# A two-block model on one core: the convolved stage with features on the partitions, norm factors spread along tokens, new forget gates, shared weight units, parameters behind the first chunk

## The chip, the cores and the metric

The kernel is one program on 1 core of one Trainium2 chip. TensorE (PE) multiplies, VectorE (DVE) and ScalarE (ACT) work on its results and prepare the weights, GpSimd (POOL) and SyncE (SP) issue most of the DMAs. The metric is device microseconds from start to end of an execution. Before the change the median of 3 runs is 1928.38 us (1926.94 to 1928.7).

## The reference, cut to what matters

A sequence of 256 tokens with 1024 features passes through two layers of a first block and two layers of a second. All data is float32.

- A layer of the first block: RMS norm, a projection to 3072 columns, attention in two kinds (4 differential heads, 8 plain heads), a projection back, and then the **convolved stage**: `u = causal_dwconv(rms_norm(x) @ w_up)`, with three taps along the tokens for each of 2 x 2816 features, split into gate and up, and `x + (silu(g) * up) @ w_down`.
- A layer of the second block: a plain gated stage (`x + 0.5 * (silu(h @ w_gate) * (h @ w_up)) @ w_down`, 2816 wide), a mixer (queries, keys, values, a recurrent unit, gates) and a second plain gated stage. In the mixer eight columns of the projection are the **forget gates**: `log_f = log_sigmoid(h @ w_f + b_f)`, one number for each token and head.

The RMS norm is `x * rsqrt(mean(x*x) + eps) * g`. The kernel multiplies `x` by `g` ahead of the product and by the token's factor (`rstd`) behind it.

## The kernel before, in words

**Products.** Every large product is done in three passes of a rounded format: an operand is split into a rounded part (`_hi`) and what is left (`_lo`), and `three` (L449 to L452) issues hi x hi, hi x lo and lo x hi into one PSUM region. 304 weight units of 1 MB stream in by DMA through three slots of `raw` (`slot` and its callers, L306 to L330); ACT rounds each half unit to `w_hi` (`hi`, L1240 to L1250) and DVE subtracts to `w_lo` (`lo`). There are six half slots; `part_done` of the half unit six back frees one. PE waits for `lo_ready`.

**Orientation.** `quarter` holds 128 tokens x 128 features of the normed input as the stationary operand and streams 512 weight columns; tokens are on the partitions of the result, and a chunk of 512 features takes two banks, one for each half of the tokens. A chunk's product is 16 tiles x 3 matmuls, in four parts. `narrow` does the last chunk of a stage (256 features, 48 matmuls of 256 columns) from a unit of its own, one for gate and one for up.

**The convolved stage** (`ffn_conv` on each engine). Six steps `j`: gate chunk, up chunk, down product of the step before. The gate chunk leaves PSUM on ACT times `rstd` (`copy_gate`, L1395), the up chunk on DVE (`copy_up`, L2176). PE transposes both so that features lie on the partitions (`turn_conv`, L557: 88 transposes in a layer). ACT takes bias and last tap from the transposed bank (`main`, L1405), DVE adds the two others (`taps`, L2188), then ACT's silu, DVE's product, and a hi and a lo for the down product.

**The plain stage** (`ffn_plain`) has silu on ACT and the product on DVE with tokens on the partitions, and transposes the product alone (`turn_prod`, L546).

**The forget gates** (`forget_logits`): for each half of the tokens and each of 8 feature tiles three matmuls with the input as the stationary operand and 8 weight columns streaming, 48 in a layer, between two parts of the mixer's first chunk.

**Stage borders.** `turn_x` (L511) transposes `x` into banks, ACT's `norm_hi` (L1265) and DVE's `norm_lo` (L2035) scale and split it. The first four tiles are turned at the end of a stage, four more at the start of the next. ACT also squares `x` (`squares_x`, L1274).

**The start.** Parameters lie in rows, are loaded by 15 small DMAs and turned on PE (`turn_params`, L918).

**Order.** Nothing is scheduled at run time. The order of every engine's queue is written out by hand, call by call; an engine works through its queue in order, so a call that waits holds back all behind it.

Of the kernel before, what the change touches and what calls it, by code (L numbers as in the profile page):

```python
# [6 lines left out]
F32 = mybir.dt.float32  # L7
# [6 lines left out]
P = 128  # L14
# [30 lines left out]

C1_ATTN, C1_FFN, C1_SUB, C1_QK, C1_CONV, C1 = 0, 8, 16, 17, 21, 197
C2_FFN1, C2_MIX, C2_FFN2, C2_BREST, C2_QN, C2_KN = 0, 8, 16, 40, 72, 73
C2_CB, C2_BA, C2_BX, C2_LAM, C2_CONV, C2_POS, C2 = 74, 82, 90, 98, 106, 138, 146

K_ID, K_TRI, K_ONEU, K_MASK, K_N = 0, 128, 256, 512, 768  # L50
# [36 lines left out]
def build_program(nc, a, out):  # L87
    with ExitStack() as ctx:
# [23 lines left out]
        wf_hi = sb("wf_hi", [P, LAYERS, KT, H2], F32R)  # L112
        wf_lo = sb("wf_lo", [P, LAYERS, KT, H2], F32R)
# [28 lines left out]
        us = stage[:, 1024:2048].rearrange("p (t c) -> p t c", t=TB)  # L142
# [6 lines left out]
        def staged(n):  # L149
# [43 lines left out]
        gs_ready, us_ready, turned_c = sem("gs_ready"), sem("us_ready"), sem("turned_c")  # L193
# [17 lines left out]
        f_done, f_abs, f_exp, f_ready, f_summed, f_copied, decay_ready = (  # L211
            sem("f_done"), sem("f_abs"), sem("f_exp"), sem("f_ready"), sem("f_summed"), sem("f_copied"),
# [14 lines left out]
        rel_done, rel_ready, wf_rounded, lam_sum, lam_exp, lam_in, lam_log = (  # L227
            sem("rel_done"), sem("rel_ready"), sem("wf_rounded"), sem("lam_sum"), sem("lam_exp"), sem("lam_in"),
# [8 lines left out]
        def half0(where):  # L237


            block, layer = where  # L240
            return 23 * layer if block == 1 else 23 * LAYERS + 50 * layer
# [48 lines left out]
        def conv_banks(j):  # L290

            return (C, E) if j == 0 else (A, B)

# [3 lines left out]
        def _(sp):  # L297
# [23 lines left out]
            def narrow(u, w, col):  # L321

                slot(u, w.rearrange("(k p) m -> p k m", p=P)[:, :, col:col + 256], KT)
# [4 lines left out]
            def ffn(u0, gate, up, up_col, down):  # L328
                for j in range(STEPS):
# [4 lines left out]
                    else:  # L334
                        narrow(u0 + ug, gate, CW * j)
                        narrow(u0 + uu, up, up_col + CW * j)
# [40 lines left out]
        def _(pool):  # L377
            nc.gpsimd.memset(eps[:, :], EPS).then_inc(eps_set, 1)
            pool.dma_start(onehot, a["const_onehot"]).then_inc(ld_rel, 16)
# [68 lines left out]
        def _(pe):  # L448
# [39 lines left out]
            def narrow(u, banks, t):  # L488

                pe.wait_ge(lo_ready, 2 * u + 2)  # L490
                for k in range(KT):
                    s, c = (2 * u + k // 4) % NH, 256 * (k % 4)
                    mm = three(bank[banks + t][:, 0:256], r_hi[:, k, t * P:(t + 1) * P], r_lo[:, k, t * P:(t + 1) * P],
                               w_hi[:, s, c:c + 256], w_lo[:, s, c:c + 256], k == 0, k == KT - 1)
                    if t and k % 4 == 3:
                        mm.then_inc(part_done, 1)
                if t == 0:
                    mm.then_inc(half_done, 1)

# [50 lines left out]
            def turn_conv(f, j, up, b):  # L550

                src, ready = (us, us_ready) if up else (gs, gs_ready)
                pe.wait_ge(ready, 12 * f + 2 * j + 2)
                for i in range(2):
                    for t in range(TB):
                        c = (2 * b + i) * P
                        mm = pe.transpose(bank[conv_banks(j)[up] + b][:, i * SEQ + t * P:i * SEQ + (t + 1) * P],  # L557
                                          src[:, t, c:c + P], ident)
                mm.then_inc(turned_c, 1)
# [7 lines left out]
            def ffn_plain(where, n, f, u0):  # L567
                def gate_part(j, i):
# [3 lines left out]
                    if j == STEPS - 1:  # L572
                        free(i)
# [88 lines left out]
            def ffn_conv(where, n, f, u0):  # L662
                def chunk_part(j, up, i):
                    def free(t):
# [3 lines left out]
                        elif j > 1:  # L668
                            pe.wait_ge(conv_done, 22 * f + 4 * (j - 1) + 2 * up + t + 1)
# [2333 lines left out]
```

## Time and profile before

| | |
|---|---|
| runs, median (range) | 1928.38 us (1926.94 to 1928.7) |
| profiled execution | 1928.72 us, span 1926.9 us, mean granted clock 0.993 |
| PE busy | 1892.6 us, 98% |
| DVE busy | 1200.8 us, 62% |
| ACT busy | 1094.6 us, 57% |
| POOL busy | 39.7 us, 2% |
| DMA | 340.86 MB, mean 177 GB/s |

The span is what the trace covers; 1.8 us of the execution lie outside it. A matmul's duration in the trace runs on beyond the start of the next, since they are pipelined: what one costs is the time from its start to the next one's start.

### The profile page before, as it was taken

How to read it: one execution, taken by the hardware profiler on the slowest of the kernel's cores; microseconds unless marked ns; L12 is line 12 of the kernel's file. 1: busy time of each engine (PE TensorE's matmuls, PEld its weight loads, DVE VectorE, ACT ScalarE, POOL GpSimd, SP SyncE). 2: the span in 40 equal slices, each digit the busy share in tenths (PEclk: the TensorE clock that was granted, in tenths of full speed). 3: DMA queues.
4: the chain of work that ended last, by engine and by line, in shares of the span. 5: the costliest groups of instructions: out<-in, count | busy, mean ns of one | idle time of the engine just before them, and what ended most of it. 6: DMA issues, size and time to landing. Idle time of an engine off the chain costs nothing.

```text
span 1926.9 us, 23554 instructions
## 1 busy us (share of the span) xinstructions
PE 1892.6 (98%) x9148; PEld 1575.3 (82%) x9148; DVE 1200.8 (62%) x1767; ACT 1094.6 (57%) x1590; POOL 39.7 (2%) x61
## 2 busy tenths in 40 slices
PE   7999999989999999999999999999999999999999
PEld 6878888878888888888878788888888887888888
DVE  6767768576777655457865554454454686664544
ACT  6766555775646534459864544454444796545442
POOL 2000000000000000000000100000000001000000
PEclk9999999999999999999999999999999999999999
DMA  6535445445554555544555555455553445544553
GB/s 220 186 131 197 154 174 197 153 150 167 186 208 156 183 197 192 175 144 167 179 204 175 175 198 195 168 188 207 178 185 122 174 163 198 187 166 172 204 191 108
DMA packets 157578, 340.86 MB, mean 177 GB/s; under 512 B 5990, under 2 KB 18891, under 8 KB 156955
## 3 DMA queue, kind: packets, MB, share of 16 engines
q1 hardware_dynamic: 154208, 327.24, 49.0%
q0 software_dynamic: 2800, 11.91, 2.0%
q8 instruction: 73, 1.20, 0.3%
q14 instruction: 38, 0.31, 0.0%
q10 hardware_dynamic: 459, 0.20, 0.0%
HBM read 338.24 MB, written 1.09 MB: 176 GB/s over the span
## 4 chain that ended last, share of the span: by engine, by line
PE 89%; DVE 5%; ACT 2%; DMA 2%; issue 1%; POOL 1%; DVEq 0%; ACTq 0%; POOLq 0%
PE bank L450 28%; PE bank L452 27%; PE bank L451 27%; DVE w_lo L2011 2%; PE bank L557 1%; PE bank L546 1%; PE bank L772 1%; DMA t<-by_key 1%; PE bank L1027 1%; ACT w_hi L1250 1%; DMA raw<-in_ffn_w_gate 1%; ACT tmp L1530 1%; PE bank L511 1%; DVE tmp L2347 0%; PE bank L816 0%
## 5 line engine op out<-in xcount | busy, mean ns | idle before, releaser
L2011 DVE TENSOR_TENSOR w_lo<-raw,w_hi 128x1024 fp32r<-128x1024 f32 x620 | 730.2, 1220 | 216.6 <-ACT w_hi L1250 210.3
L1250 ACT ACTIVATE w_hi<-raw 128x1024 fp32r<-128x1024 f32 x620 | 631.3, 1055 | 303.1 <-PE bank L452 172.7
L450 PE MATMUL bank<-w_hi,r_hi 128*128 128x512 f32 (+1 forms) x1792 | 691.2, 386 | 1.5 <-DVE r_lo L2035 1.4
L452 PE MATMUL bank<-w_hi,r_lo 128*128 128x512 f32 (+1 forms) x1792 | 680.6, 380 | 0.0
L451 PE MATMUL bank<-w_lo,r_hi 128*128 128x512 f32 (+1 forms) x1792 | 679.9, 379 | 0.0
L450 PEld LDWEIGHTS bank<-w_hi,r_hi 128*128 128x128 f32 x1792 | 339.1, 189 | 67.0 <-issue 2.5
L452 PEld LDWEIGHTS bank<-w_hi,r_lo 128*128 128x128 f32 x1792 | 338.7, 189 | 64.3
L451 PEld LDWEIGHTS bank<-w_lo,r_hi 128*128 128x128 f32 x1792 | 339.2, 189 | 60.1
L450 PE MATMUL bank<-w_hi,z_hi 128*128 128x512 f32 x656 | 259.0, 395 | 1.7 <-DVE w_lo L2011 1.7
L452 PE MATMUL bank<-w_hi,z_lo 128*128 128x512 f32 x656 | 256.0, 390 | 0.0
L451 PE MATMUL bank<-w_lo,z_hi 128*128 128x512 f32 x656 | 255.4, 389 | 0.0
L450 PEld LDWEIGHTS bank<-w_hi,z_hi 128*128 128x128 f32 x656 | 123.2, 188 | 27.1 <-DVE w_lo L2011 2.1
L452 PEld LDWEIGHTS bank<-w_hi,z_lo 128*128 128x128 f32 x656 | 123.1, 188 | 26.1
L451 PEld LDWEIGHTS bank<-w_lo,z_hi 128*128 128x128 f32 x656 | 123.3, 188 | 24.4
L2073 DVE SCALAR_TENSOR_TENSOR qk<-bank,rstd,stage 128x512 f32<-128x512 f32 (+1 forms) x48 | 33.9, 706 | 132.4 <-PE bank L452 131.8
L2188 DVE SCALAR_TENSOR_TENSOR qk<-bank,par,qk 128x254 f32<-128x254 f32 (+1 forms) x176 | 72.6, 475 | 63.3 <-ACT qk L1405 63.0
L1284 ACT ACTIVATE z_hi<-bank 128x512 fp32r<-128x512 f32 x44 | 25.5, 589 | 148.7 <-PE bank L546 148.7
L1296 ACT ACTIVATE stage<-bank,rstd 128x512 f32<-128x512 f32 (+1 forms) x48 | 31.2, 650 | 102.0 <-PE bank L452 101.9
L1405 ACT ACTIVATE qk<-bank,par 128x256 f32<-128x256 f32 x88 | 43.9, 561 | 67.9 <-PE bank L557 67.9
L2011 DVE TENSOR_TENSOR z_lo<-bank,z_hi 128x512 fp32r<-128x512 f32 x52 | 35.2, 687 | 58.1 <-ACT z_hi L1284 53.4
L2035 DVE SCALAR_TENSOR_TENSOR r_lo<-bank,par,r_hi 128x256 fp32r<-128x256 f32 x80 | 34.4, 478 | 43.9 <-ACT r_hi L1265 43.7
L450 PE MATMUL bank<-w_hi,y_hi 128*128 128x512 f32 x128 | 50.9, 398 | 0.4 <-issue 0.4
(208 smaller groups left out, 1399.0 us busy)
## 6 DMA issues: line engine op xcount, KB each, us to landing
raw<-in_w_in SPq DMA_DIRECT2D x79, 1024.0 KB, 5.3
raw<-in_w_up SPq DMA_DIRECT2D x44, 1024.0 KB, 5.3
raw<-in_ffn_w_gate SPq DMA_DIRECT2D x44, 1024.0 KB, 5.2
raw<-in_ffn_w_up SPq DMA_DIRECT2D x44, 1024.0 KB, 5.7
raw<-in_ffn_w_down SPq DMA_DIRECT2D x44, 1024.0 KB, 5.3
raw<-in_w_down SPq DMA_DIRECT2D x22, 1024.0 KB, 5.0
raw<-in_w_out SPq DMA_DIRECT2D x16, 1024.0 KB, 5.0
raw<-in_w_o_rnn SPq DMA_DIRECT2D x8, 1024.0 KB, 5.0
```

The lines of the kernel that those rows point to most:

```text
L450: pe.matmul(out_, lh, rh, start=start, stop=False, skip_group_check=True)
L451: pe.matmul(out_, lh, rl, start=False, stop=False, skip_group_check=True)
L452: return pe.matmul(out_, ll, rh, start=False, stop=stop, skip_group_check=True)
L511: mm = pe.transpose(x_tile(where, n, k)[:, t * P:(t + 1) * P], x[:, t, k * P:(k + 1) * P], ident)
L1250: A_(w_hi[:, n % NH, :], raw[:, u % NS, HALF * h:HALF * (h + 1)], ACT.Copy).then_inc(hi_ready, 1)
L1284: A_(z_hi[:, tiles, :], src, ACT.Copy).then_inc(g_hi_ready, 1)
L1296: A_(gs[:, t, 0:width], bank[pair_of(j) + t][:, 0:width], ACT.Silu, scale=rstd[:, t:t + 1]).then_inc(silu_ready, 1)
L1405: last = A_((cg, cu)[up][:, tile, :], bank[conv_banks(j)[up] + b][:, i * SEQ:(i + 1) * SEQ], ACT.Identity, bias=kinds[:, 0, up, 4 * j + ti ...
L2011: return V.tensor_tensor(dst, src, hi.bitcast(F32), ALU.subtract)
L2035: V.scalar_tensor_tensor(out=r_lo[:, k, :], in0=x_tile(where, n, k), scalar=gain[:, k:k + 1], in1=r_hi[:, k, :].bitcast(F32), op0=ALU.mult ...
L2073: V.scalar_tensor_tensor(out=prod[:, t, 0:width], in0=bank[pair_of(j + 1) + t][:, 0:width], scalar=rstd[:, t:t + 1], in1=gs[:, t, 0:width] ...
L2188: ks.append(own.link(V.scalar_tensor_tensor(out=dst, in0=bank[conv_banks(j)[up] + b][:, i * SEQ:(i + 1) * SEQ - tap], scalar=kinds[:, kind ...
```

## The change

- In the convolved stage `quarter_rows` takes the place of `quarter` and `narrow`: 128 weight columns are the stationary operand and the 256 tokens stream. A bank holds two feature tiles x 256 tokens; a chunk is 32 tiles x 3 matmuls. The result has features on the partitions, so `turn_conv`, `copy_gate` and `copy_up` go.
- `rstd` is one number for each token and lies on partitions; `spread_factors` turns it so that it lies along the tokens on every partition (2 transposes), DVE copies that to SBUF, and DVE's `scale` multiplies each bank by it into the staging tile. ACT's `main` and DVE's `taps` read that tile and not PSUM.
- The last chunk's gate and up columns share two units in all six gated stages (`pairs`: two DMAs for a unit), and are computed as one 512-column chunk. `narrow` goes.
- The forget gates' 8 weight columns are the first of a stationary operand of 128 columns (what follows in memory fills the rest), the 256 tokens stream: 24 matmuls in a layer. ACT copies 8 rows, PE turns them back in two transposes. They stand one part later in the queue.
- At the start `turn_params(0)` stands behind the first four tiles of `x`, the others partly behind the first chunk, and the rounding of the first weights ahead of the norm.
- At the stage borders the order of squares, norm tiles, weight halves and first products is changed, and many calls in the attention, the mixer and the plain stage change places with neighbours.

```diff
+SHARED = {f0 + 28 + half for half in range(2) for f0 in ...}
-    return (6 * j - 2, 6 * j, 6 * j + 2) if j < STEPS - 1 else (28, 29, 30)
+    return (6 * j - 2, 6 * j, 6 * j + 2) if j < STEPS - 1 else (28, 28, 30)
...
+            def quarter_rows(u, half, n, banks, ready=None, free=None):
+                def tile(m, kk):
+                    k = 4 * half + kk
+                    s, c = (2 * u + kk // 2) % NH, CW * (kk % 2) + P * m
+                    return three(bank[banks + m // 2][:, SEQ * (m % 2):SEQ * (m % 2) + SEQ], w_hi[:, s, c:c + P],
+                                 w_lo[:, s, c:c + P], r_hi[:, k, :], r_lo[:, k, :], k == 0 and m % 2 == 0, k == KT - 1)
+                if half == 0:
+                    pe.wait_ge(lo_ready, 2 * u + n + 1)
+                    for kk in (2 * n, 2 * n + 1):
+                        for m in range(4):
+                            mm = tile(m, kk)
+                    mm.then_inc(part_done, 1)
+                else:
...
+                    for kk in range(4):
+                        for m in (2 * n, 2 * n + 1):
+                            mm = tile(m, kk)
+                        if n and kk % 2:
+                            mm.then_inc(part_done, 1)
+                    if n == 0:
+                        mm.then_inc(half_done, 1)
+
+            def spread_factors(where, n, f):
+                pe.wait_ge(rstd_ready, norm_at(where, n) + 1)
+                for t in range(TB):
+                    mm = pe.transpose(bank[C][:, t * P:(t + 1) * P], rstd[:, t:t + 1].broadcast_to([P, P]), ident)
+                mm.then_inc(spread, 1)
...
                 def forget_logits():
+                    for k in range(KT):
+                        c = (l * KT + k) * H2
+                        mm = three(bank[C][:, 0:256], wf_hi[:, c:c + P], wf_lo[:, c:c + P], r_hi[:, k, :], r_lo[:, k, :],
+                                   k == 0, k == KT - 1)
+                    mm.then_inc(f_done, 1)
-                        for k in range(KT):
-                            mm = three(bank[C][:, t * H2:(t + 1) * H2], r_hi[:, k, t * P:(t + 1) * P],
-                                       r_lo[:, k, t * P:(t + 1) * P], wf_hi[:, l, k, :], wf_lo[:, l, k, :],
...
+                def copy_factors():
+                    dve.wait_ge(spread, f + 1)
+                    own.link(V.tensor_copy(factors, bank[C][:, 0:SEQ]))
+                def scale(j, up, b):
...
+                        dve.wait_ge(conv_main, 22 * f + 4 * (j - 1) + 2 * up + b + 1)
+                    V.tensor_tensor((gf, uf)[up][:, b, :, :], src[:, :].rearrange("p (i s) -> p i s", i=2),
+                                    factors.unsqueeze(1).broadcast_to([P, 2, SEQ]), ALU.mult).then_inc(scaled, 1)
...
 # DVE, convolved stage, steps 2 to 4
                 for j in range(2, STEPS - 1):
+                    scale(j, 0, 0)
                     lo(uj, 0)
-                    prod_lo(j - 1, 0)
                     lo(uj, 1)
                     lo(uj + 1, 0)
                     lo(uj + 1, 1)
+                    prod_lo(j - 1, 0)
+                    prod_lo(j - 1, 1)
+                    lo(uj + 2, 0)
+                    scale(j, 0, 1)
+                    lo(uj + 2, 1)
+                    scale(j, 1, 0)
+                    lo(uj + 3, 0)
+                    scale(j, 1, 1)
+                    lo(uj + 3, 1)
                     taps(j, 0, 0)
...
 # PE, end of the convolved stage
                 last_half(u0, f, 1, 1, 0)
+                turn_next(where, n, 0)
                 last_half(u0, f, 1, 1, 1)
-                turn_next(where, n, 0)
...
 # PE, start of a plain and of a convolved stage
+                gate_part(0, 0)
                 turn_x(where, n, 4)
-                gate_part(0, 0)
...
 # ACT, start of a plain stage
-                hi(u0 + 2, 0)
+                squares_x(where, n, 0)
                 norm_hi(where, n, 0)
                 norm_hi(where, n, 1)
                 norm_hi(where, n, 2)
+                hi(u0 + 2, 0)
                 norm_hi(where, n, 3)
...
 # PE, start of the program
                 x_first(0)
-                turn_params(0)
                 x_first(1)
                 x_first(2)
                 x_first(3)
+                turn_params(0)
                 turn_params(1)
```

## Rows read from the trace of the kernel before

**Rows 1.** The page: busy time of each engine, share of the span, instructions
```profile
PE 1892.6 (98%) x9148; PEld 1575.3 (82%) x9148; DVE 1200.8 (62%) x1767; ACT 1094.6 (57%) x1590; POOL 39.7 (2%) x61
PE 89%; DVE 5%; ACT 2%; DMA 2%; issue 1%; POOL 1%; DVEq 0%; ACTq 0%; POOLq 0%
```
**Rows 2.** Timeline, PE: start us, duration us, what; first and 46th 512-column matmul of a run
```profile
199.80 0.39 PE L452 MATMUL bank<-w_hi,r_lo 128*128 128x512 f32 x1
...
210.00 0.39 PE L452 MATMUL bank<-w_hi,r_lo 128*128 128x512 f32 x1
```
**Rows 3.** Timeline, PE: first and 53rd 256-column matmul of a run
```profile
300.31 0.28 PE L450 MATMUL bank<-w_hi,r_hi 128*128 128x256 f32 x1
...
306.55 0.28 PE L451 MATMUL bank<-w_lo,r_hi 128*128 128x256 f32 x1
```
**Rows 4.** Timeline, PE: eight transposes and what follows
```profile
210.23 1.03 PE L557 MATMUL bank<-cst,stage 128*128 128x128 f32 x8
...
211.33 0.40 PE L451 MATMUL bank<-w_lo,r_hi 128*128 128x512 f32 x1
```
**Rows 5.** Groups by form, PE, whole span: count, busy us, mean ns
```profile
L557 PE MATMUL bank<-cst,stage 128*128 128x128 f32 x176 | 23.4, 272 | 0.0
```
**Rows 6.** Timeline, PE: forget gates of layer 0, the first, and products after
```profile
840.00 0.17 PE L450 MATMUL bank<-wf_hi,r_hi 128*128 128x8 f32 x1
...
846.72 0.77 PE L450 MATMUL bank<-w_hi,r_hi 128*128 128x512 f32 x1
...
851.32 0.39 PE L450 MATMUL bank<-w_hi,r_hi 128*128 128x512 f32 x1
```
**Rows 7.** Timeline, PE: forget gates of layer 1, first, and products after
```profile
1482.55 0.17 PE L450 MATMUL bank<-wf_hi,r_hi 128*128 128x8 f32 x1
...
1490.04 0.77 PE L450 MATMUL bank<-w_hi,r_hi 128*128 128x512 f32 x1
...
1495.70 0.39 PE L451 MATMUL bank<-w_lo,r_hi 128*128 128x512 f32 x1
```
**Rows 8.** Windows: stretch, busy us (count) of PE, PEld, DVE, ACT, POOL, clock, DMA
```profile
843.70:850.50 6.80, 6.80 (x25) 6.03 (x25) 3.57 (x6) 0.78 (x1) 0.00 (x0) 0.50 0.11 16
1485.40:1495.60 10.20, 10.20 (x36) 9.04 (x37) 3.94 (x6) 1.06 (x1) 0.00 (x0) 0.50 0.24 72
1096.30:1099.70 3.40, 3.40 (x10) 2.52 (x9) 0.00 (x0) 3.35 (x6) 0.00 (x0) 0.50 0.59 230
138.00:331.00 193.00, 192.48 (x945) 161.36 (x943) 139.70 (x204) 112.45 (x159) 0.00 (x0) 1.00 0.51 178
```
**Rows 9.** Groups by form, DVE, whole span
```profile
L2011 DVE TENSOR_TENSOR w_lo<-raw,w_hi 128x1024 fp32r<-128x1024 f32 x620 | 730.2, 1220 | 216.6 <-ACT w_hi L1250 210.3
L2011 DVE TENSOR_TENSOR z_lo<-bank,z_hi 128x512 fp32r<-128x512 f32 x52 | 35.2, 687 | 58.1 <-ACT z_hi L1284 53.4 <-ACT z_hi L1837 4.4
```
**Rows 10.** Timeline from the start, PE, DVE and ACT; in brackets the wait
```profile
11.06 0.62 PE L918 MATMUL bank<-cst,tmp 109*128 109x109 f32 x2 [4.38 <-DMA tmp<-in_conv_w]
11.73 0.37 DVE L2433 COPY par<-bank 128x202 f32<-128x202 f32 x1 [2.67 <-PE bank L918]
13.84 1.26 DVE L2035 SCALAR_TENSOR_TENSOR r_lo<-bank,par,r_hi 128x256 fp32r<-128x256 f32 x3
16.28 0.79 PE L450 MATMUL bank<-w_hi,r_hi 128*128 128x512 f32 x1
```
**Rows 11.** Timeline, ACT and PE, start of a plain stage
```profile
1092.94 1.06 ACT L1250 ACTIVATE w_hi<-raw 128x1024 fp32r<-128x1024 f32 x1 [1.80 <-DMA raw<-in_ffn_w_up]
1095.03 0.41 PE L511 MATMUL bank<-cst,x 128*128 128x128 f32 x2 [2.09 <-DVE r_lo L2035]
```
**Rows 12.** Timeline, PE: start of a stage behind a convolved one; two waits in the attention
```profile
330.31 1.58 PE L511 MATMUL bank<-cst,x 128*128 128x128 f32 x8 [0.52 <-DVE r_lo L2035]
...
89.83 0.44 PE L816 MATMUL bank<-cst,tmp 128*128 128x128 f32 x2 [0.90 <-DVE tmp L2365]
...
415.85 1.09 PE L844 MATMUL bank<-cst,stage 128*128 128x128 f32 x8 [1.51 <-DVE stage L2321]
```

More of the change, by code:

```diff
@@ L44 @@
 UNITS = LAYERS * (U1 + U2)
+SHARED = {f0 + 28 + half for half in range(2) for f0 in
+          [U1 * n + U_WIN + U_WOUT for n in range(LAYERS)]
+          + [LAYERS * U1 + U2 * n + m for n in range(LAYERS) for m in (0, U_FFN + U_MIX)]}
 C1_ATTN, C1_FFN, C1_SUB, C1_QK, C1_CONV, C1 = 0, 8, 16, 17, 21, 197
@@ L141, in build_program @@
         gs = stage[:, 0:1024].rearrange("p (t c) -> p t c", t=TB)
-        us = stage[:, 1024:2048].rearrange("p (t c) -> p t c", t=TB)
+        gf, uf = (stage[:, 1024 * n:1024 * (n + 1)].rearrange("p (b i s) -> p b i s", b=2, i=2) for n in range(2))
+        factors = t4[:, 0:SEQ]
         cg, cu, cp = qk[:, 0:4, :], qk[:, 4:8, :], qk[:, 8:12, :]
@@ L240, in half0, with landed @@
             block, layer = where
-            return 23 * layer if block == 1 else 23 * LAYERS + 50 * layer
+            return 22 * layer if block == 1 else 22 * LAYERS + 48 * layer
+        def landed(u):
+            n = 0
+            for b in range(u % NS, u + 1, NS):
+                n += 2 if b in SHARED else 1
+            return 16 * n
         def norm_at(where, n):
@@ L334, in ffn @@
                     else:
-                        narrow(u0 + ug, gate, CW * j)
-                        narrow(u0 + uu, up, up_col + CW * j)
+                        for half in range(2):
+                            pairs(u0 + ug + half, gate, up, CW * j, up_col + CW * j, half)
                     if j:
@@ L960, in _ @@
                 scores(where, 0)
+                turned(2)
                 part(3, 2)
+                scores(where, 1)
                 part(3, 3)
-                turned(2)
-                scores(where, 1)
-                part(4, 0)
                 scores(where, 2)
                 turn(where, 0)
+                part(4, 0)
                 part(4, 1)
+                scores(where, 3)
                 part(4, 2)
+                turn(where, 1)
+                turned(3)
                 part(4, 3)
-                turned(3)
-                turn(where, 1)
-                scores(where, 3)
                 part(5, 0)
@@ L1161, in _ @@
                 part(7, 3)
+                part(8, 0)
                 turned(5)
-                part(8, 0)
                 part(8, 1)
+                forget_sums()
                 part(8, 2)
-                forget_sums()
-                turned(6)
                 part(8, 3)
                 part(9, 0)
-                scores(where, 0)
                 part(9, 1)
@@ L2097, in ffn_plain @@
                 lo(u0 + 3, 1)
+                deviation(where, n)
                 lo(u0 + 4, 0)
+                product(0, 0)
+                product(0, 1)
                 lo(u0 + 4, 1)
@@ L2216, in ffn_conv @@
                 norm_lo(where, n, 7)
+                deviation(where, n)
+                copy_factors()
                 lo(u0 + 2, 0)
-                deviation(where, n)
+                scale(0, 0, 0)
                 lo(u0 + 2, 1)
@@ L2243, in ffn_conv @@
                 lo(u0 + 9, 0)
+                prod_lo(0, 0)
+                product(0, 1)
+                prod_lo(0, 1)
+                taps(1, 0, 1)
                 lo(u0 + 9, 1)
+                scale(1, 1, 0)
+                scale(1, 1, 1)
                 lo(u0 + 10, 0)
                 lo(u0 + 10, 1)
-                taps(1, 0, 0)
-                prod_lo(0, 1)
-                copy_up(1, 0)
-                lo(u0 + 11, 0)
-                taps(1, 0, 1)
-                copy_up(1, 1)
                 taps(1, 1, 0)
-                lo(u0 + 11, 1)
                 taps(1, 1, 1)
```

815 lines of the change are left out of this document (384 added, 431 removed).

## The prediction, made before the changed kernel was run

> **What bounds the kernel now.** I read the page first: PE is busy 98% of the span and the chain that ended last is PE for 89% [rows 1]. Busy is no proof that PE works at its rate, so I went to its timeline next and took starts, not durations. From the first to the 46th of a run of 512-column matmuls 10.20 us pass in 45 steps, 0.2267 us each [rows 2]; in the narrow chunk 52 steps of 256 columns take 6.24 us, 0.120 us each [rows 3]. Each holds its columns at the full clock of 2.4 GHz (213 and 107 ns) and 13 ns more. In a whole convolved stage PE is busy 192.48 of 193.00 us at a granted clock of 1.00, while DVE has 139.70 and ACT 112.45 us of work [rows 8]. So this kernel is a string of PE instructions at a fixed step, and a change is worth what it takes out of that string, plus the few places where the string stands still or the clock is down. Those places I found last, by windows and waits: the start, the forget gates, the stage borders, the attention.
>
> **The change part by part.** All against the profiled execution: span 1926.9 us, 1928.7 with the 1.8 us around it, which is 0.3 above the median of 1928.4.
>
> *Transposes out.* 176 in both layers [rows 5]. Eight and the start of regular stepping after them: the next matmul but one starts at 211.33, 1.10 us after the first at 210.23 [rows 4]; of these 0.227 belong to the matmul between, 0.87 for eight, 0.109 each. 176 x 0.109 = 19.2 us out. In come 2 x 2 of `spread_factors`, 0.4 us.
>
> *Twice as many matmuls of half the length.* A full chunk was 48 x 0.2267 = 10.88 us and becomes 96 x 0.120 = 11.52: 0.64 more. Ten full chunks in a layer (gate and up, five steps), two layers: +12.8 us. I take the step of the narrow chunk [rows 3] although there the normed input was held and weights streamed; both come from SBUF in 128 x 128 pieces in the same format. Were weights dearer to hold, the load's time could show: the bound is 0.2267 a matmul, twice the cost, which I hold for excluded, since a load of 128 columns precedes every matmul in both rows. Below the 0.107 us of its columns it can't go.
>
> *The last chunk of a stage.* In the convolved stage 96 matmuls of 256 columns stay 96. In the four plain stages 96 x 0.120 become 48 x 0.2267: 0.64 each, -2.6 us.
>
> *Forget gates.* Here the trace shows what the counts hide. In layer 0 the 8-column matmuls start at 840.00, and the 13th large matmul behind them, by which the step is 0.227 again, at 851.32 [rows 6]. Less 12 x 0.2267 that makes 8.6 us for a product of 8 columns. In layer 1: 1482.55 to the 14th at 1495.70, less 13 steps, 10.2 us [rows 7]. The granted clock stands at 0.50, the lower level of 1.2 GHz, for 6.8 and 10.2 us there [rows 8], it fell during the 8-column matmuls and not in a gap: PE counts as busy in all of the stretch. After the change 24 x 0.120 plus two small transposes at 0.109, 3.1 us a layer, streaming 256 columns as the narrow chunk does, which ran at full clock [rows 3]. 18.8 - 6.2 = 12.6 us out. The wait of the turn for ACT's copy has a part of the next chunk (2.7 us) before it.
>
> The Trainium skill, page "TensorE: Matmul & The Clock Gate", section "Why this matters for your kernels", names gaps in which PE is idle between bursts as what throws the clock back. By that, matmuls without a gap should not have lowered it, and some other cause would remain after the change; this is rival B below. The trace speaks against it: no gap of PE lies ahead of the fall.
>
> *Start.* PE waits 4.38 us for the convolution's parameters, with three tiles of `x` queued behind, and the first weight product starts at 16.28 [rows 10]. After: those tiles go first, the parameters are turned at the same 11.06, copied by 12.1 [rows 10], and four `norm_lo` at 0.42 (1.26 for three) follow; `turn_x(7)` needs the fourth. 12.1 + 1.7 = 13.8: 2.5 us earlier. Against it, ACT does three weight halves ahead of four norm tiles, 3.2 us by the 1.06 of [rows 11], which might be missed later: between 5.2 gained (all from 11.06 to 16.28) and 3.2 lost. I take -2.5.
>
> *Borders.* At 1095.03 PE had waited 2.09 us for the first norm tile, because ACT stood on a weight half whose DMA was late (1.80 us, and 1.06 to do it) ahead of the norm; the clock then fell for 3.4 us [rows 8, 11]. The norm now goes first. About 1.5 us of wait go; of the 3.4 us at half clock (1.7 lost) I count half, sum -2.4; bounds 0 and -3.8. Behind the two convolved stages the first `turn_x` hides behind a last part: 0.52 us each [rows 12], -1.0; the six other borders keep their wait.
>
> *Attention and mixer.* Of waits like 0.90 and 1.51 us [rows 12] there are about four a layer in the first block. Softmax steps start earlier and the group scale is ahead of other DVE work. I can't add this up; between 5 us gained in both layers and 3 lost I take -1.5.
>
> *What DVE takes on.* `scale` replaces `copy_up` and also the gate copy of ACT: 22 x 0.69 for 8.5 us of `copy_up` in a layer, so 146 of some 190 us, still short of PE. What counts is what stands behind it. `scale(j, 0, 0)` waits for the third part of the gate chunk, and `lo(uj, 0)`, needed by the next chunk's first part, stands behind it: 0.69 + 1.22 [rows 9] = 1.9 us against the 24 x 0.120 = 2.9 us of the fourth part. Cover 1.0 us, less semaphores. `copy_factors` in step 0 is alike: 0.4 + 1.2. ACT's last weight half of a step stands behind two silus that wait for taps; by the same prices it comes about 2 us early. At the end of the stage the chain scale, main, taps, silu, product, hi, lo has 10.9 us of down product and needs some 10. I put +1.5 for small misses in 12 steps; bounds 0 and 6.
>
> Sum: -19.2 + 0.4 + 12.8 - 2.6 - 12.6 - 2.5 - 2.4 - 1.0 - 1.5 + 1.5 = **-27.1**; 1928.7 - 27.1 = 1901.6, against the median 1901.3. I say **1901 us**.
>
> **The rivals.**
>
> *B. The clock falls at the same places for another reason.* For it: it also fell at a border and in the attention, where no 8-column work was. Against it: there PE had just waited. Price: half of the 6.8 and 10.2 us at 0.50 [rows 8], 8.5 us back: 1910.
>
> *C. DVE's queue sets the step of the convolved stage: slower than before.* Place: `lo` behind `scale`. For it: eight taps and four scales a step now depend on each other across ACT and DVE, and in the old trace ACT and DVE already waited for one another; cover is 1 us. If each chunk loses a whole scale and a weight half, 1.9 us x 22 chunks = 42 us on top of 1900: 1942. It decides from 28.6 / 22 = 1.3 us a chunk. Against it: work of 146 in 190 us leaves 2 us a chunk to catch up.
>
> *D. Only what is counted comes.* Reorderings at the start, borders and attention give nothing and cost 3 us in new waits, the convolved stage loses 3: 1928.4 - 21.2 + 6 = 1913.
>
> *E. The half-length matmuls step at more than 0.120* with four regions in turn in two banks. At 0.125: 1920 matmuls x 0.005 = 10 us, 1911. The 13 ns above the columns is the same at both lengths, which speaks against a further term.
>
> **How the numbers follow.** Forecast 0.70 (1892 to 1908), B 0.06, C 0.04, D 0.14, E 0.06. The range 1892 to 1913 takes in B, E and D's edge; the low end is the start and attention at their better bounds (-3 and -3) and no misses. What a measurement can tell is 0.2%, 4 us: slower 0.04 (C and a little of the unforeseen), same 0.01, faster 0.95, since counted terms alone are five times that.
>
> **What would show it.** No transposes between the up parts; 256-column steps of 0.120 in gate and up chunks. 24 matmuls for the forget gates and a clock of 1.00 after them. First weight product near 13.8. PE without gaps in steps 2 to 4 of the convolved stage, which then takes about 189 us; if C holds, PE waits for `w_lo` there, released by DVE. The prediction is wrong if the clock falls within the long 256-column runs, or if a convolved stage takes over 192 us.

## The result, and the profile after

The changed kernel takes **1899.13 us** (median of 4 runs, 1898.58 to 1901.29), against 1927.92 (1926.94 to 1928.7) for the kernel before on the same chip: ratio 0.9853, 95% interval 0.9836 to 0.987, faster by 28.8 us. The forecast was 1901 us. The profiled execution has a span of 1897.4 us (before 1926.9) and a mean granted clock of 1.00 (before 0.993).

The page after, busy time of each engine and the chain that ended last, answers to [rows 1]:

```profile
PE 1869.0 (98%) x9700; PEld 1582.5 (83%) x9700; DVE 1215.5 (64%) x1789; ACT 1084.8 (57%) x1564; POOL 44.1 (2%) x63
PE 90%; DVE 4%; ACT 3%; issue 1%; DMA 1%; ACTq 0%; DVEq 0%
```

PE has 552 more instructions and is busy 24 us less. As before, the busy share says nothing: 98% both times. The starts of the matmuls do. PE's timeline of the changed kernel, the first, 53rd and 97th 256-column matmul of step 2's gate and up chunks, answers to [rows 3]:

```profile
192.24 0.28 PE L470 MATMUL bank<-r_hi,w_hi 128*128 128x256 f32 x1
...
198.47 0.28 PE L471 MATMUL bank<-r_lo,w_hi 128*128 128x256 f32 x1
...
203.75 0.28 PE L470 MATMUL bank<-r_hi,w_hi 128*128 128x256 f32 x1
```

52 steps in 6.23 us and 96 in 11.51 us: 0.120 each, as in the narrow chunk. Windows of the changed kernel (stretch, busy us and count of PE, PEld, DVE, ACT, POOL, clock, DMA share, GB/s): the convolved stage, then the forget gates of layer 0 with what follows, then layer 1. They answer to [rows 8]:

```profile
132.30:321.40 189.10, 188.52 (x1337) 177.51 (x1336) 146.00 (x213) 107.32 (x145) 0.00 (x0) 1.00 0.54 181
838.00:846.00 8.00, 8.00 (x46) 6.67 (x45) 5.38 (x11) 4.10 (x8) 0.00 (x0) 1.00 0.41 133
1460.00:1480.00 20.00, 20.00 (x106) 16.94 (x105) 12.85 (x20) 11.08 (x16) 0.00 (x0) 1.00 0.42 134
```

The stage is 4.0 us shorter, DVE's 146.00 us fit in, and in neither stretch around the forget gates does the clock fall to 0.50. PE's timeline of the changed kernel, forget gates of layer 0, answers to [rows 6]:

```profile
836.14 0.28 PE L470 MATMUL bank<-r_hi,wf_hi 128*128 128x256 f32 x1
...
838.85 0.28 PE L472 MATMUL bank<-r_hi,wf_lo 128*128 128x256 f32 x1
838.96 0.71 PE L780 MATMUL bank<-cst,stage 128*128 128x128 f32 x5
```

24 matmuls in 2.82 us. The start, PE's timeline with the wait in brackets, answers to [rows 10]:

```profile
5.53 1.97 PE L519 MATMUL bank<-cst,x 128*128 128x128 f32 x8 [2.50 <-DMA x<-in_x]
11.09 0.62 PE L926 MATMUL bank<-cst,tmp 109*128 109x109 f32 x2 [3.59 <-DMA tmp<-in_conv_w]
12.70 0.56 PE L926 MATMUL bank<-cst,tmp 88*128 88x88 f32 x2 [0.98 <-DMA tmp<-in_conv_w]
14.61 0.78 PE L470 MATMUL bank<-w_hi,r_hi 128*128 128x512 f32 x1
15.19 0.63 PE L471 MATMUL bank<-w_lo,r_hi 128*128 128x512 f32 x1
15.61 0.45 PE L472 MATMUL bank<-w_hi,r_lo 128*128 128x512 f32 x1
15.90 0.39 PE L470 MATMUL bank<-w_hi,r_hi 128*128 128x512 f32 x1
```

The first weight product comes 1.67 us earlier than in the kernel before. From 15.19 to 15.61 a 512-column product steps 0.42 us, about twice the 0.2267 of [rows 2], which is the lower level of the clock; from 15.90 on the step is the full clock's. Two products stand at the low step here and three in the kernel before; of the executions below, the one with the parameters first has none and the one with the copy ahead has eight in a row. So a start's length in one execution holds some chance. The 41st weight product starts at 24.53, before the change at 26.92.

**Where the time went.** I cut both traces at the first `turn_x` of each stage (PE's `cst,x` group) and took the stage lengths, in us. Plain 1.0 and 2.0 are the first and second plain stage of the second block's layer 0, plain 1.1 and 2.1 those of layer 1; the last one ends with PE's last matmul.

| stage | before | after | difference |
|---|---|---|---|
| up to and with attention 0 | 135.62 | 132.41 | -3.21 |
| convolved 0, 1 | 193.13, 193.14 | 189.13, 189.15 | -4.00, -3.99 |
| attention 1 | 119.03 | 119.97 | +0.94 |
| plain 1.0 (behind convolved 1) | 188.01 | 189.13 | +1.12 |
| mixer 0, 1 | 262.90, 264.57 | 255.03, 255.74 | -7.87, -8.83 |
| plain 2.0 (behind mixer 0) | 190.96 | 187.72 | -3.24 |
| plain 1.1, 2.1 | 188.28, 188.04 | 188.02, 187.92 | -0.26, -0.12 |

The sum is -29.5, as the spans have it. After the change the first `turn_x` stands ahead of the last part of the convolved stage, and that part takes 0.68 us: 0.68 of each convolved stage's 4.0 is only counted to the stage behind it. Put back where the work belongs, it is -3.3 for each convolved stage, +0.3 for attention 1 and +0.4 for plain 1.0. Besides the falls in [rows 8] the trace of the kernel before has one more, in attention 0, at the layer-0 twin of the wait of 1.51 in [rows 12]; the changed kernel's execution has none there. Window of the kernel before:

```profile
103.00:106.40 3.40, 3.25 (x16) 2.76 (x16) 2.80 (x9) 2.82 (x8) 0.00 (x0) 0.50 0.02 5
```

### The profile page after: what moved, and what is told of

The parts are those of the page before. It is cut to its first block, busy times and chain, and to the rows that moved or that the text cites. A ratio compares the mean times of both kernels' runs of the same rounds, so it can differ in the third digit from the quotient of the medians.

```text
span 1897.4 us, 24659 instructions
## 1 busy us (share of the span) xinstructions
PE 1869.0 (98%) x9700; PEld 1582.5 (83%) x9700; DVE 1215.5 (64%) x1789; ACT 1084.8 (57%) x1564; POOL 44.1 (2%) x63
## 4 chain that ended last, share of the span: by engine, by line
PE 90%; DVE 4%; ACT 3%; issue 1%; DMA 1%; ACTq 0%; DVEq 0%
PE bank L470 28%; PE bank L472 28%; PE bank L471 28%; DVE w_lo L2016 1%; PE bank L554 1%; DMA raw<-in_w_in 1%; PE bank L780 1%; PE bank L519 1%; ACT w_hi L1268 1%; PE bank L824 1%; PE bank L803 1%; PE bank L868 1%; DMA tmp<-in_conv_w 0%; PE bank L1035 0%; ACT tmp L1527 0%
## 5 line engine op out<-in xcount | busy, mean ns | idle before, releaser
L470 PE MATMUL bank<-w_hi,r_hi 128*128 128x512 f32 x1344 | 534.3, 398 | 4.3 <-DVE r_lo L2040 3.4
L472 PE MATMUL bank<-w_hi,r_lo 128*128 128x512 f32 x1344 | 524.4, 390 | 0.0
L471 PE MATMUL bank<-w_lo,r_hi 128*128 128x512 f32 x1344 | 523.7, 390 | 0.0
L470 PEld LDWEIGHTS bank<-w_hi,r_hi 128*128 128x128 f32 x1344 | 252.7, 188 | 59.5 <-issue 4.4
L470 PE MATMUL bank<-r_hi,w_hi 128*128 128x256 f32 x704 | 199.9, 284 | 1.2 <-DVE r_lo L2040 1.2
L472 PE MATMUL bank<-r_hi,w_lo 128*128 128x256 f32 x704 | 199.3, 283 | 0.0
L471 PE MATMUL bank<-r_lo,w_hi 128*128 128x256 f32 x704 | 199.3, 283 | 0.0
L470 PEld LDWEIGHTS bank<-r_hi,w_hi 128*128 128x128 f32 x704 | 135.1, 192 | 2.0 <-issue 1.6
L471 PEld LDWEIGHTS bank<-r_lo,w_hi 128*128 128x128 f32 x704 | 135.1, 192 | 0.3
L472 PEld LDWEIGHTS bank<-r_hi,w_lo 128*128 128x128 f32 x704 | 135.1, 192 | 0.0
```

What stands on the lines that cost most here:

```text
L470: pe.matmul(out_, lh, rh, start=start, stop=False, skip_group_check=True)
L471: pe.matmul(out_, lh, rl, start=False, stop=False, skip_group_check=True)
L472: return pe.matmul(out_, ll, rh, start=False, stop=stop, skip_group_check=True)
```

## The experiments

Each was run four times on the same chip as the kernel before; all but the third start from the changed kernel. Given are medians with their range; the ratio is to the kernel before, with its 95% interval. Stage lengths are from one profiled execution each.

**The forget gates: 8 columns streaming, or something else?** The first puts the old product in the new place.

```diff
-    mm = three(bank[C][:, 0:256], wf_hi[:, c:c + P], wf_lo[:, c:c + P], r_hi[:, k, :], r_lo[:, k, :], ...)
+    mm = three(bank[C][:, t * H2:(t + 1) * H2], r_hi[:, k, t * P:(t + 1) * P],
+               r_lo[:, k, t * P:(t + 1) * P], wf_hi[:, c:c + H2], wf_lo[:, c:c + H2], ...)
-    forget_turn(); forget_copy()
```

> The changed kernel with the forget gates' product back in its old form: 48 matmuls of 8 columns in a row in a layer, all else as changed. Theory A (streaming 8 columns for several microseconds lowers the clock although PE has no gap): granted clock 0.50 for 6 to 10 us in each mixer, and the time goes up by 9 to 13 us, to 1908 to 1912. Rival B (only gaps lower the clock, the fall had another cause): clock 1.00 throughout, 48 x 0.112 us less the 3.1 us of the new form, twice: +4.5 us, 1903.6.

Measured 1912.59 us (1909.17 to 1916.87), ratio 0.9928 (0.9907 to 0.9949); mixers 260.76 and 258.77 us, 5.7 and 3.0 above the changed kernel's. The profiled execution is the fastest of the four; the slower ones have lower mean granted clocks (0.994 to 0.996 against 0.997). The clock falls in both layers, with PE busy in every part of the stretch and no wait on PE in the 14 us ahead. In layer 0 the matmuls step 0.112 us up to the 32nd and 0.213 behind it; in layer 1 the fall comes at the end of the 48. Windows of this kernel:

```profile
839.80:846.60 6.80, 6.80 (x31) 6.51 (x31) 1.21 (x4) 2.07 (x5) 0.00 (x0) 0.50 0.38 143
1478.10:1481.50 3.40, 3.40 (x14) 3.11 (x14) 1.29 (x4) 2.15 (x5) 0.00 (x0) 0.51 0.22 86
```

The second does the same 48 matmuls in four groups of 12 with large products between.

```diff
+    forget_logits((0,))    # behind part(0, 3); (1,) behind part(1, 0), (2,) behind part(1, 1), (3,) behind part(1, 2)
```

> As the kernel with 8-column matmuls in the changed kernel, but the 48 stand in four groups of 12, each behind another part of 24 large matmuls. Theory A (the length of the stretch of 8-column work counts): a group is 1.3 us, the clock stays at 1.00, and only the counted cost is left, +4.5 us, 1903.6. Rival (48 such matmuls lower the clock wherever they stand): 1908 to 1912, clock 0.50 near them.

1905.19 us (1903.71 to 1907.15), ratio 0.9883 (0.9867 to 0.9898). Mixers 257.61 and 257.57, 2.6 and 1.8 above the changed kernel's, where 2.2 each were counted, and no fall in either layer. This execution does have one in attention 1, at 430.3, where the stage takes 121.51 us; the two timed runs with a mean granted clock of 1.000 took 1903.71 and 1904.21. Window of this kernel over the four groups:

```profile
835.00:850.00 15.00, 15.00 (x96) 13.42 (x95) 8.34 (x16) 8.05 (x11) 0.00 (x0) 1.00 0.47 157
```

So the same instructions lower the clock in one block and leave it in four. What lowered it is the unbroken run of 8-column matmuls. No idle PE is needed.

The third adds the new forget gates alone to the kernel before.

```diff
 # before.py
+    mm = three(bank[C][:, 0:256], wf_hi[:, c:c + P], wf_lo[:, c:c + P], r_hi[:, k, :], r_lo[:, k, :], ...)
+    part(0, 3); forget_turn()          # PE
+    stage_chunk(0, 0); forget_copy()   # ACT
```

> The kernel before with the new forget gates alone (24 matmuls of 256 columns and two small transposes a layer), every order as before. Theory: 18.8 us become 6.2, so 12.6 us less, 1915.3, no fall of the clock in the mixers. Rival (the mixers' further gain of some 4 us in the changed kernel is an after-effect of the clock that stays up): 16 to 17 us less, 1911.5.

1916.51 us (1914.96 to 1917.67), ratio 0.994 (0.9926 to 0.9955): 10.3 below the kernel before, and 12.6 were counted. The mixers fall by 4.7 and 6.4 us (5.5 and 7.1 counted); in both layers PE meets a new wait, which takes 2.6 us of the gain. Timeline, PE, of this kernel:

```profile
858.37 0.50 PE L454 MATMUL bank<-w_hi,r_hi 128*128 128x512 f32 x1 [1.16 <-DVE w_lo L2033]
...
1494.12 0.50 PE L454 MATMUL bank<-w_hi,r_hi 128*128 128x512 f32 x1 [1.40 <-DVE w_lo L2033]
```

**The order in the mixer.** The changed kernel's mixers are 3.2 and 2.4 us shorter still than the third's. This one puts back the old lists of all three engines in the mixer and keeps the new gates.

```diff
-    forget_logits() ... turned(1); lru_linear(1); turned(2) ... gate_part(0, 0); scores(where, 0)
+    forget_logits(); forget_turn(); lru_linear(0); turned(1); lru_linear(1) ... scores(where, 0); gate_part(0, 0)
```

> The changed kernel with the mixers' queues in the order of before (the new forget gates in the old place, between the third and fourth part), all else as changed. Theory (the further gain of about 4 us in the two mixers came from the new order, chiefly scores and transposes spaced out in the attention): 2 x 2 us slower, 1903. Rival (it came with the clock): 1899, the same.

1913.32 us (1911.24 to 1914.26), ratio 0.9923 (0.9908 to 0.9938); mixers 262.76 and 258.33, 7.7 and 2.6 above the changed kernel's. The waits that return in the attention part are those of before. PE's timeline of the kernel before:

```profile
967.37 0.70 PE L795 MATMUL bank<-qk 128*128 128x256 f32 x2 [1.35 <-DVE nmax L2347]
...
989.52 0.50 PE L450 MATMUL bank<-w_hi,z_hi 128*128 128x512 f32 x1 [0.92 <-DVE w_lo L2011]
```

and of this one:

```profile
957.96 0.70 PE L803 MATMUL bank<-qk 128*128 128x256 f32 x2 [1.35 <-DVE nmax L2369]
...
980.47 0.50 PE L470 MATMUL bank<-w_hi,z_hi 128*128 128x512 f32 x1 [1.25 <-DVE w_lo L2016]
```

The changed kernel has neither. In layer 1 PE's waits add up to 3.6 us against 0.9, which is the 2.6: 1.9 in the attention part, 1.18 at 1490.13 behind the forget gates. Layer 0 has the wait behind the gates too, and longer. Timeline of this kernel, ACT and PE:

```profile
845.06 1.06 ACT L1268 ACTIVATE w_hi<-raw 128x1024 fp32r<-128x1024 f32 x1 [6.61 <-DMA raw<-in_w_in]
...
851.41 0.50 PE L470 MATMUL bank<-w_hi,r_hi 128*128 128x512 f32 x1 [2.46 <-DVE w_lo L2016]
```

DVE's reading of the gates, in its old place, waits for the turned gates and holds back a `lo`; that frees its `raw` slot late, the DMA starts late, and PE waits 2.46 us. The clock then falls for 3.4 us. So with the new gates DVE's reading of them had to move too. How much its old place costs is not fixed: 2.46 and 1.18 us here, 1.16 and 1.40 and no fall in the third experiment, which has the same order there. Why layer 0 fares so much worse here is not shown. In this execution plain 2.0, whose lists were not touched, takes 189.28 us, 1.6 more than in the changed kernel.

**The convolved stage back.**

```diff
-    quarter_rows(...); spread_factors(...); scale(j, up, b)
+    quarter(...); turn_conv(f, j, up, b); copy_gate(j, t); copy_up(j, t)   # shared units kept
```

> The changed kernel with the convolved stage back in its old form (tokens on the partitions, 88 transposes a layer, gate copy on ACT, up copy on DVE), the shared units kept. Theory by count: a layer gets 9.6 us of transposes and loses 0.2 of factors, ten chunks of 11.52 and one more become 10.88 (7.0): +2.3 us a layer, 4.7 in all, 1903.8. Rival (the count misses something in the new form, such as relief of ACT): over 8 us slower, 1907 or more. Rival (the new form is no better): 1899.

1908.84 us (1905.96 to 1912.0), ratio 0.9904 (0.9887 to 0.9922). Both convolved stages are 3.7 us longer than the changed kernel's; counted were 2.4 (3.0 less the 0.64 that a last chunk of 512 columns saves the old form). Of the other 1.3 some 0.6 lie at the stage's border, where PE waits 0.44 us for `x`; the last 0.7 I can't place. The profiled execution has 4.3 us more in attention 1 (124.2 us), where PE waits 2.47 us and the clock falls. Two of the four timed runs have a mean granted clock of 1.000; they took 1905.96 and 1906.6, which the two stages explain alone. Window of this kernel:

```profile
434.90:441.70 6.80, 6.03 (x14) 4.77 (x15) 0.93 (x3) 0.26 (x1) 0.00 (x0) 0.51 0.10 37
```

**The order in the first block's attention back.**

```diff
-    scores(where, 3); turn(where, 1); turned(3)   ...   hi(u0 + 4, 0); lambda_exps()
+    turned(3); turn(where, 1); scores(where, 3)   ...   lambda_exps(); hi(u0 + 3, 1)   # and the start's order
```

> The changed kernel with the queues of the first block's attention stages, start of the program among them, in the order of before. Theory: all gain is at the start: layer 0's stage longer by 2.5 to 3.3 us, layer 1's stage by -0.3 to 0.3; 1902. Rival (the attention orders brought something too): layer 1's stage longer by 1 us or more, 1904.

1902.18 us (1900.7 to 1902.95), ratio 0.9868 (0.9854 to 0.9883). The first stage is 2.6 us longer. Its first weight product starts at 15.55, 0.9 later, and seven products instead of two stand at the low step, which is chance in part; the 41st starts at 26.92 against 24.53, and from there to the stage's end it is 108.1 us against 107.9. Attention 1 is 119.91, 0.06 shorter. So the new lists gain at the start and next to nothing in the attention itself. The other 1.4 us of this execution are in plain 2.0.

**The parameters first at the start.**

```diff
+    turn_params(0)        # PE: back ahead of the other tiles of x
```

> The changed kernel with one call back in its old place: the turn of the first parameters behind the first tile of x, so that three tiles wait for their DMA. Theory (the chain parameters, norm, first product sets the start, and the tiles' place ahead of the wait matters): the three tiles come 0.7 us behind the parameters and ACT's norm chain with them: 0.5 to 1.5 us slower. Rival (the start hangs on the rounding of the first weights): no change.

1900.46 us (1898.22 to 1903.03), ratio 0.9861 (0.9846 to 0.9875). The first weight product starts at 14.37, not later than the 14.61 of the changed kernel, yet the stage is 0.8 us longer, with a wait of 0.64 at 66.68 that the changed kernel has not. The timed runs don't tell the two kernels apart; what this one move is worth stays open.

**How much room does DVE have?** `scale` is done twice, then four times; the repeats write the same values.

```diff
+    for again in range(1):    # range(3) in the second
+        own.link(V.tensor_tensor((gf, uf)[up][:, b, :, :], ..., ALU.mult)); own.wait()
```

> The changed kernel with each of DVE's 44 multiplications by the norm factors done twice (the second overwrites the first with the same values), about 0.8 us more each with the wait between. Theory (the convolved stage is PE's; cover of a weight half behind a multiplication is 1 us): within 2 us of 1899. Rival C (DVE's queue already sets the step): 44 x 0.8 = 35 us slower.

1909.61 us (1908.39 to 1910.18), ratio 0.9912 (0.9895 to 0.9928): 10 us on top, where I expected at most 2. DVE has 160.18 us of work in a stage of 193, which is not a full engine. The stages are 3.7 and 5.2 us longer, and in the first it is two waits. PE's timeline of this kernel:

```profile
200.47 0.39 PE L470 MATMUL bank<-r_hi,w_hi 128*128 128x256 f32 x1 [1.98 <-DVE w_lo L2016]
...
320.66 0.50 PE L470 MATMUL bank<-w_hi,z_hi 128*128 128x512 f32 x1 [1.40 <-DVE z_lo L2016]
```

They stand in step 2 and at the stage's end, where the last product's chain must come through; the other steps absorb 2.8 us of extra DVE work each. The second stage has the same two waits, and behind its first one the clock falls for 3.4 us at 516.5, which makes the 5.2. The rest of the 10 us is attention 1, which is 1.7 us longer, with a fall of 3.4 us at 434.6 behind waits that the changed kernel has as well.

> The same with each multiplication done four times, about 2.4 us more each. Theory: DVE's work in a convolved stage becomes 147 + 22 x 2.4 = 200 us against PE's 189, and the cover of 1 us is gone: 15 to 60 us slower, PE waiting for the low weight halves. Rival (there is much more slack than I count): under 10 us slower.

1966.97 us (1966.39 to 1968.27), ratio 1.0212 (1.0197 to 1.0228): slower than before. Convolved stages 222.4 and 223.5. Window and PE's waits (us in all, times, longest) of this kernel there:

```profile
132.00:354.00 222.00, 196.44 (x1335) 182.78 (x1335) 190.89 (x279) 107.59 (x146) 0.00 (x0) 0.97 0.45 156
```

```profile
PE bank L470 <- DVE w_lo L2016: 19.6, 9, 4.1
PE bank L470 <- DVE z_lo L2016: 5.2, 1, 5.2
```

**The borders.** In the changed kernel ACT starts the stage behind a convolved one with the squares of `x`, which need the last addition. Timeline, ACT and PE, of the changed kernel:

```profile
631.37 1.06 ACT L1292 ACTIVATE t<-x 128x1024 f32<-128x1024 f32 x1 [3.59 <-DVE x L2053]
...
632.55 1.20 ACT L1283 ACTIVATE r_hi<-bank,par 128x256 fp32r<-128x256 f32 x3
...
633.69 0.47 PE L470 MATMUL bank<-w_hi,r_hi 128*128 128x512 f32 x1 [1.31 <-DVE r_lo L2040]
```

```diff
-    squares_x(where, n, 0); norm_hi(where, n, 0) ... hi(u0 + 2, 0); norm_hi(where, n, 3)
+    norm_hi(where, n, 0) ... norm_hi(where, n, 3); squares_x(where, n, 0); hi(u0 + 2, 0)
```

> The changed kernel with the squares of x behind the first four norm tiles at the start of the second block's layers (as before) and ahead of them elsewhere. Theory (there ACT waits for the add of x with the squares at its head, 631.37 to 632.5, and PE stands for 1.31 us): the wait of PE at 633.7 falls from 1.31 to 0.4 or so and that at 1264.5 from 0.92 to 0.5: 1.3 us less, 1897.8. Rival (the norm then waits for the transposes just as long): the same.

1901.0 us (1899.76 to 1902.66), ratio 0.9861 (0.9845 to 0.9877). Plain 1.0 is 189.52, 0.4 longer, and plain 1.1 188.98, 1.0 longer: the first wait halves, and a second comes. The weight half now stands behind norm and squares; that this makes the second wait is my reading, and the last experiment, which leaves the weight half where it was, has no second wait. PE's timeline of this kernel:

```profile
634.90 0.47 PE L470 MATMUL bank<-w_hi,r_hi 128*128 128x512 f32 x1 [0.69 <-DVE r_lo L2045]
...
638.94 0.47 PE L470 MATMUL bank<-w_hi,r_hi 128*128 128x512 f32 x1 [0.84 <-DVE r_lo L2045]
```

**Two orders mended.** In attention 1 of the changed kernel ACT waits for a late DMA with the copy of PE's operand behind it. Its timeline, ACT and PE:

```profile
426.79 1.06 ACT L1268 ACTIVATE w_hi<-raw 128x1024 fp32r<-128x1024 f32 x1 [3.36 <-DMA raw<-in_w_up]
...
427.76 0.85 ACT L1540 ACTIVATE tmp<-bank 128x384 f32<-128x384 f32 x2
...
428.66 0.66 PE L868 MATMUL bank<-tmp,v 128*64 128x256 f32 x4 [1.23 <-ACT tmp L1540]
...
430.49 0.50 PE L470 MATMUL bank<-w_hi,y_hi 128*128 128x512 f32 x1 [0.95 <-DVE y_lo L2016]
```

```diff
+    copy_turned(where, 7); hi(u0 + 16, 0); att_high(where, 7); hi(u0 + 16, 1)
-    hi(u0 + 16, 0); copy_turned(where, 7); hi(u0 + 16, 1); att_high(where, 7)
```

> The changed kernel with two calls moved on ACT in the first block's attention: the copy of the last turned probabilities and the high part of the last attention output each stand ahead of a weight half and not behind it. Theory (at 426.79 ACT had waited 3.36 us for a late weight unit with the copy, ready since 424.6, behind it, so that PE stood 1.23 us, and 0.95 us more for the low part; these two gaps are also what lets the clock fall near 430 in some executions): the 1.23 us gap goes in both layers and the second shrinks, 1.3 to 2.5 us less in all, 1897; attention stage of layer 1 at 118 to 119 us, no fall of the clock there. Rival (PE then waits for the weight halves that come later): the same time, gaps moved behind the output parts.

1897.58 us (1897.16 to 1900.98), ratio 0.9856 (0.9841 to 0.9871). Attention 1 takes 118.73 us, 1.2 less; the wait of 1.23 is gone, that of 0.95 stays. By the timed runs it can't be told from the changed kernel (0.9853). The last adds an order at the border that keeps the weight half in its place.

```diff
+    norm_hi 0, 1, 2; hi(u0 + 2, 0); norm_hi 3; squares 0, squares 1    # ACT, n == 0
```

> The same, and at the start of the second block's layers the squares of x behind the first four norm tiles and the weight half (unlike the run with the norm before the squares, the weight half keeps its place between the third and the fourth tile). Theory (the weight half's late place held DVE's norm tiles in that run; the squares are what PE waits for in the changed kernel): stages of 188.1 and 187.6 us for 189.1 and 188.0, 1.3 us less than the run with the copy ahead alone, 1895.5. Rival: as long as the run with the copy ahead.

1897.68 us (1895.88 to 1899.1), ratio 0.9853 (0.9836 to 0.9869). Plain 1.0 and 1.1 take 188.53 and 187.58, 0.6 and 0.4 less than the changed kernel's, and PE waits half as long. Its timeline:

```profile
631.91 0.47 PE L470 MATMUL bank<-w_hi,r_hi 128*128 128x512 f32 x1 [0.69 <-DVE r_lo L2043]
```

Its span is 1895.3 against 1897.4 us, and the stages say where the 2 us come from. But the timed runs, against the kernel before of the same chip, give 0.9853 for both kernels: that it is the better one is not shown.

## Why the prediction was right, point by point

The prediction's terms against what the stage table gives, in us:

| term | predicted | measured |
|---|---|---|
| convolved stages: transposes, factors, double matmuls, misses | -4.5 | -6.6 |
| forget gates | -12.6 | -11.1 (the mixers of the third experiment) |
| order in attention and mixer | -1.5 | -5.6 in the mixers (the rest of their -16.7), +0.3 in attention 1 |
| start | -2.5 | -3.2, attention 0 included |
| four plain stages: last chunks -2.6, late norm and clock -2.4, borders -1.0 | -6.0 | -3.2 |
| sum | -27.1 | -29.5 |

That the sum comes out so near is luck in part: the order in the mixers gave 4 us more than counted and the plain stages 3 less.

**Right in mechanism and size.** The convolved stages give 6.6 us where 6.0 were counted without misses, and a 256-column step is 0.120 us with the weights held as with the weights streamed, which ends E. The +1.5 for misses was not needed: PE's only wait in the stage is one of 0.6 us. Put back into the changed kernel, the old form costs 3.7 us a layer where 2.4 were counted, 0.7 of it unplaced; no run takes the transposes alone.

**The forget gates** were the large hidden term, and reading starts instead of counts found it. B is shown false by three kernels: the fall comes back with the 8-column block, stays away when the block is cut in four, and goes when only the gates are changed. What the prediction called 8.6 and 10.2 us for the product lay mostly in it: 6.7 and 7.5 us pass until the first large product, 1.9 and 2.7 are lost on the large products behind. By the Trainium skill's "TensorE: Matmul & The Clock Gate", section "Why this matters for your kernels", gaps in which PE is idle between bursts of matmuls throw the clock back. The falls at 435.0 (convolved stage back) and at 852.2 (old mixer order) stand behind waits of 2.47 and 2.46 us, which is the same kind of place; the two at the forget gates of [rows 8] do not, since PE was busy throughout.

**C** did not happen, but its mechanism exists. The prediction took DVE's slack as 2 us in each chunk. The doubled scale shows that it is not an even sum: 14 us more work in a stage made PE wait 3.4 us, at two places. With the extra work of the fourfold scale, three times that of the doubled one, the kernel ends slower than before; where between the two it turns was not run.

**D** falls, though part of it came true. The orders at the borders behind the convolved stages and in attention 1 gave nothing: the first `norm_lo` stands behind DVE's last addition, so hiding the first `turn_x` moved the wait rather than took it out. DVE's timeline of the changed kernel at the first of these borders:

```profile
322.72 0.69 DVE L2053 SCALAR_TENSOR_TENSOR x<-bank,x 128x512 f32<-128x512 f32 x1 [0.51 <-PE bank L472]
323.33 2.06 DVE L2040 SCALAR_TENSOR_TENSOR r_lo<-bank,par,r_hi 128x256 fp32r<-128x256 f32 x5
```

**Mis-sized.** The mixers' order was in a common -1.5 and gave 5.6 us. Against the third experiment the changed kernel's mixers lack 2.8 us of waits on `nmax` and `w_lo` in the attention part and the 2.6 behind the gates. The kernel before has 4.5 us of the first kind (1.35 and 0.92 in layer 0, 1.40 and 0.80 in layer 1); they stood in its trace and were not priced, since [rows 12] shows only waits of the first block.

The plain stages were counted at -6.0 and gave -3.2. The shared last chunk was to bring 0.64 in each; plain 1.1 and 2.1 are 0.26 and 0.12 shorter. In plain 2.1 PE's first wait is 0.06 longer than before the change, and two products behind `turn_x` step 0.35 and 0.34 us instead of 0.227: the weight load of the second waits for DVE's norm tile. The busy time doesn't show that, only the starts do. Timeline, PE, of the changed kernel:

```profile
1714.86 0.40 PE L472 MATMUL bank<-w_hi,r_lo 128*128 128x512 f32 x1
1715.21 0.50 PE L470 MATMUL bank<-w_hi,r_hi 128*128 128x512 f32 x1
1715.55 0.39 PE L471 MATMUL bank<-w_lo,r_hi 128*128 128x512 f32 x1
```

These are 0.24 us, and all four plain stages have them. (Plain 1.1 has a first wait 0.3 longer besides; the kernel before loses 0.28 us there in its own way, at 1465.) The shared chunk also makes PE turn its operands in four groups more. That costs almost nothing, as PE's timeline of the changed kernel shows for a group of two:

```profile
321.54 0.38 PE L519 MATMUL bank<-cst,x 128*128 128x128 f32 x2
321.67 0.47 PE L470 MATMUL bank<-w_hi,z_hi 128*128 128x512 f32 x1
321.99 0.39 PE L471 MATMUL bank<-w_lo,z_hi 128*128 128x512 f32 x1
```

From 321.54 to 321.99 it is 0.45 us, less one product 0.22 for two transposes, 0.11 each, as in a group of eight [rows 4]. The product behind a group steps 0.32, but the group's last transpose only 0.03. Over all groups of both traces one of eight costs 0.89 us and one of four 0.454, so a split costs 0.02. In plain 2.1 that leaves 0.14 of the missing 0.52 us unexplained.

The start's first product came at 14.61 and not 13.8: PE waits 0.98 us for the second parameters' DMA, which I had not in the sum. The stage gains 3.2 all the same, 2.4 of it by the 41st product.

The late norm at 1095 came out in size: plain 2.0 gives -3.24 for a counted -3.0 (-2.4 and a last chunk). By its parts it is a wait of 2.09 that became 0.58 and a fall of 3.4 us, 1.7 lost, that is gone whole where half was counted; the last chunk then gave nothing. And it is not shown that the norm's new place did it. Two kernels with that place unchanged have the wait back, the one with the old mixer order and the one with the old attention order (189.16 us, 2.06 at 1080.48). PE's timeline of the changed kernel:

```profile
1076.43 0.47 PE L470 MATMUL bank<-w_hi,r_hi 128*128 128x512 f32 x1 [0.58 <-DVE r_lo L2040]
```

and of the kernel with the old mixer order:

```profile
1085.89 0.47 PE L470 MATMUL bank<-w_hi,r_hi 128*128 128x512 f32 x1 [2.13 <-DVE r_lo L2040]
```

So something ahead of the stage decides it; I take it to be the time at which the weights' DMAs come, but no run tests that.

## What to carry to other kernels

On an engine that is 98% busy, price a change by the step from start to start of a long run, and look at the granted clock of every place where small instructions stand: 48 matmuls of 8 columns cost 8.6 and 10.2 us a layer, 1.9 and 2.7 of it on the large products behind them. When a stage has a fifth of an engine's time left, ask at which instruction the slack is least. And an order by hand is a whole: the changed kernel with the old mixer order takes 262.76 us for layer 0's mixer, 0.1 less than before any change, although the same gates in the same order gained 4.7 us in the kernel before.

## What the runs showed of the hardware that I had not expected

A block of 48 eight-column matmuls, all busy and back to back, takes PE's clock from 2.4 to 1.2 GHz (granted 0.50) for 3.4 to 10.2 us. The same 48 in four blocks of 12 with 512-column products between leave it at 1.00. How long it stays low differs between layers and kernels: 6.8 and 10.2 us in the kernel before, 6.8 and 3.4 in the first experiment; nothing here says why.

Waits of 1.2 to 1.4 us and of 0.95 near 430 were followed by a fall of 3.4 us in three of the profiled executions and by none in the changed kernel's, with 1.23 and 0.95. Waits of 0.90, 0.67 and 1.51 around 90 to 103 were followed by a fall in the kernel before and by none in the third experiment, which has the same three. I can't tell what decides it.

Transposes of 128 columns in float32 step 0.109 us, and cutting a group of eight in two costs 0.02 us. The first weight products of most executions step 0.43 us, the lower level of the clock, two of them in the changed kernel's and eight in a row in the one with the copy ahead, and 0.227 from then on.
